# Opening transfers put in an order of their own, and the last norm of a diffusion trunk layer split over ScalarE and VectorE, on eight cores

## Time and profile before

| what | us |
|---|---|
| runs of the kernel before, median of 3 | 1055.67 (1051.9 to 1056.66) |
| the profiled execution | 1051.73 |
| its span on the slowest core (core 6) | 1049.8 |
| spans of the eight cores | 1039.6 to 1049.8 |
| PE matmul busy | 893.6 (85%) |
| DVE / POOL / ACT busy | 492.8 / 434.8 / 325.9 |

### The profile page before, as it was taken

The page is one execution under the profiler, slowest core; times in us unless marked ns, Lnnn a source line. Parts: engine busy times, 40 slices in busy tenths (PEclk is TensorE's granted clock), DMA queues, the critical chain, the costliest instruction groups (busy, mean ns, idle before and its releaser), DMA issues.

```text
span 1049.8 us, 15523 instructions; the slowest of 8 cores (1039.6 to 1049.8 us)
## 1 busy us (share of the span) xinstructions
PE 893.6 (85%) x5266; PEld 427.6 (41%) x5357; DVE 492.8 (47%) x979; ACT 325.9 (31%) x492; POOL 434.8 (41%) x411
## 2 busy tenths in 40 slices
PE   2136989877999998999989899979999999999970
PEld 1112544443444444444434444434444444444430
DVE  3134732776784227742477533322255433332380
ACT  1113745873782222762235421101112111111111
POOL 6033764312445235742576520033348633421055
PEclk9968999999999999999999999989999999999995
DMA  9995367452345668862768659986759875443027
GB/s 176 191 213 147 109 103 113 65 102 42 71 111 102 100 122 189 190 101 41 162 167 204 133 93 165 177 166 139 150 109 152 154 138 129 111 78 74 1 40 120
DMA packets 54636, 129.99 MB, mean 124 GB/s; under 512 B 5024, under 2 KB 6304, under 8 KB 54304
## 3 DMA queue, kind: packets, MB, share of 16 engines
q0 software_dynamic: 31584, 69.15, 41.7%
q1 hardware_dynamic: 22976, 59.86, 20.5%
HBM read 164.58 MB, written 16.78 MB: 173 GB/s over the span
## 4 chain that ended last, share of the span: by engine, by line
PE 58%; DMA 21%; issue 7%; DVE 6%; ACT 4%; POOL 2%; SPq 0%; DVEq 0%; POOLq 0%; ACTq 0%
PE psum L512 55%; DMA arena<-wff 6%; DMA arena<-wada 4%; DMA arena<-arena 4%; DMA arena<-xh 2%; DMA arena<-badabc 2%; DMA arena<-ctxb 2%; DMA out<-arena 1%; DVE arena L528 1%; DVE arena L524 1%; PE psum L710 1%; PE psum L676 1%; ACT arena L680 1%; ACT arena L777 1%; POOL arena L504 1%
## 5 line engine op out<-in xcount | busy, mean ns | idle before, releaser
L512 PE MATMUL psum<-arena 128*128 128x512 bf16 (+2 forms) x3704 | 806.5, 374 | 51.1 <-DVE arena L618 14.3
L512 PEld LDWEIGHTS psum<-arena 128*128 128x128 bf16 x3792 | 361.0, 99 | 472.6 <-issue 79.9
L806 POOL TENSOR_TENSOR arena<-arena 128x512 bf16<-128x512 f32 x88 | 113.6, 1302 | 187.6 <-DMA arena<-wff 149.5
L824 ACT ACTIVATE arena<-psum 128x512 f32<-128x512 f32 x88 | 52.4, 596 | 311.4 <-PE psum L512 311.4
L825 DVE TENSOR_TENSOR arena<-psum,arena 128x512 bf16<-128x512 f32 x88 | 60.8, 691 | 175.2 <-PE psum L512 166.4
L524 DVE BATCH_NORM_STATS2 arena<-arena 128x6 f32<-128x512 f32 x152 | 103.7, 689 | 73.2 <-DMA arena<-xh 31.5
L837 DVE TENSOR_TENSOR arena<-psum,arena 128x1024 f32<-128x1024 f32 x64 | 78.2, 1223 | 57.3 <-PE psum L512 57.2
L527 POOL TENSOR_TENSOR arena<-arena 128x1 f32<-128x1 f32 x84 | 51.3, 628 | 97.1 <-DVE arena L526 91.6
L749 DVE SCALAR_TENSOR_TENSOR arena<-arena,psum 128x512 f32<-128x512 f32 x64 | 43.7, 685 | 93.1 <-PE psum L512 89.4
L680 ACT ACTIVATE arena<-psum 128x1024 bf16<-128x1024 f32 x80 | 78.0, 1024 | 14.3 <-PE psum L676 12.8
L745 ACT ACTIVATE arena<-psum 128x512 f32<-128x512 f32 x64 | 38.1, 598 | 95.3 <-PE psum L512 95.2
(11 more groups left out here) (72 smaller groups left out, 566.0 us busy)
## 6 DMA issues: line engine op xcount, KB each, us to landing
arena<-wff SPq DMA_DIRECT2D x88, 256.0 KB, 4.9
arena<-wff POOLq DMA_DIRECT2D x22, 1024.0 KB, 10.8
arena<-xh SPq DMA_DIRECT2D x34, 512.0 KB, 7.0
arena<-wada POOLq DMA_DIRECT2D x24, 512.0 KB, 9.1
arena<-wc POOLq DMA_DIRECT2D x16, 768.0 KB, 8.3
arena<-arena POOLq DMA_DIRECT2D x16, 512.0 KB, 6.2
out<-ln2b SPq DMA_DIRECT2D x16, 512.0 KB, 35.6
out<-arena POOLq DMA_DIRECT2D x16, 512.0 KB, 7.0
```

Source lines behind the costliest of these rows:

```text
L512: r = e.matmul(out, lhsT=pairs[i][0], rhs=pairs[i][1], start=(i == 0), stop=(i == n - 1))
L806: G.op('pool', lambda e, fi=fi, hs=hs, stg=stg: e.tensor_tensor(out=w2[i % 5][:, fi, hs], in0=stg, in1=g2bc[:, hs], op=ALU.mult))
L824: G.op('act', lambda e: e.activation(out=sg, in_=ps[0], func=AF.Silu))
```

## The change

- The planner's prices (`cost`) and its hand-over times change for all engines, so that the order on each engine may change anywhere.
- Opening: wqk, perm and wu are issued right behind the w_ada blocks; x tiles 6 to 9 are read through the software queue; x tiles 4 and 5 no longer wait for the last w_ada block; wvb, wv, masks and wst follow. The second rope part waits for wu, the small loads and later x tiles and rope parts for wv or wst, the `wada1` blocks for wst. The context pair moves from group 0 to group 1.
- In late q and k units the permutation product goes to bank 5 (`bk_misc`) instead of banks 6 and 7.
- c2: ln1b is added by POOL instead of an accumulating DMA.
- Tail: the last accumulate is done in two half passes that also give row sums; ACT squares with the mean as bias and sums; two DVE passes apply mean, gain, scale and offset; SP stores the result. The 16 transfers that fill the output with ln2b go; ln2b is loaded once.

```diff
 def cost(self, eng, name, a, kw, out, ins):
-            return (1.0 if eng == 'pool' else 0.07)
+            return (0.8 if eng == 'pool' else 0.07)
...
-                    return 0.9
-                return 0.15 + n * 2.6 / 1200.0
-            return 0.15 + n * 1.05 / 1200.0
+                    return 0.56
+                return 0.18 + n / 472.0
+            return 0.34 + n / 1196.0
...
-                done = end + (0.2 if e == 'pe' else 0.1)
+                done = end + (0.25 if e == 'pe' else 0.15)
...
-    def qk_unit(m, hcol, n, dst, banks):
-        pq, ps = bk(banks())[:, 0:n], bk(banks())[:, 0:n]
+    def qk_unit(m, hcol, n, dst, banks, pbanks):
+        pq, ps = bk(banks())[:, 0:n], bk(pbanks())[:, 0:n]
...
-        G.op('pool', lambda e: e.dma_start(out=w, in_=ln1b, accum_op=ALU.add))
+        G.op('pool', lambda e: e.tensor_tensor(out=w, in0=w, in1=ln1b, op=ALU.add))
...
-    def tail(t):
+    def tail(t, b0):
+
         acc = xmid[t]
-        rstd, nmr = stats(acc, 1024)
-        y = y0[t % 3]
-        G.op('act', lambda e: e.activation(out=y, in_=acc, func=AF.Identity, scale=rstd, bias=nmr))
-        G.op('pool', lambda e: e.tensor_tensor(out=y, in0=y, in1=ln2g, op=ALU.mult))
-        G.finals.append(G.op('pool', lambda e: e.dma_start(out=out_d[t * 128:(t + 1) * 128, :], in_=y, accum_op=ALU.add)))
+        y = y0[t % 2]
+        s = st_i[0] % NST
+        st_i[0] += 1
+        st, mv = stt[:, s], mvr[:, s]
+        for h in range(2):
+            hs = slice(h * 512, (h + 1) * 512)
+            G.op('dve', lambda e, h=h, hs=hs: e.scalar_tensor_tensor(
+                out=acc[:, hs], in0=bk(b0 + h), scalar=1.0, in1=acc[:, hs], op0=ALU.mult, op1=ALU.add,
+                accum_out=st[:, h:h + 1]))
+        G.op('dve', lambda e: e.tensor_scalar(out=mv[:, 0:1], in0=st[:, 0:1], scalar1=st[:, 1:2], scalar2=-1.0 / D,
+                                              op0=ALU.add, op1=ALU.mult))
+        G.op('act', lambda e: e.activation(out=junk, in_=acc, func=AF.Square, bias=mv[:, 0:1], scale=1.0,
+                                           accum_out=st[:, 8:9]))
+        G.op('dve', lambda e: e.scalar_tensor_tensor(out=y, in0=acc, scalar=mv[:, 0:1], in1=ln2g, op0=ALU.add,
+                                                     op1=ALU.mult))
+        G.op('dve', lambda e: e.tensor_scalar(out=mv[:, 2:3], in0=st[:, 8:9], scalar1=1.0 / D, scalar2=EPS, op0=ALU.mult,
+                                              op1=ALU.add))
+        G.op('pool', lambda e: e.tensor_tensor(out=mv[:, 3:4], in0=mv[:, 2:3], in1=neghalf[:, 0:1], op=ALU.pow))
+        G.op('dve', lambda e: e.scalar_tensor_tensor(out=acc, in0=y, scalar=mv[:, 3:4], in1=ln2b, op0=ALU.mult,
+                                                     op1=ALU.add))
+        G.finals.append(load(out_d[t * 128:(t + 1) * 128, :], acc))
...
+    lq = cast_load(flat(wqk), wqk_d)
+    cast_load(perm, perm_d)
+    lu = cast_load(flat(wu), wu_d)
...
     a1_pair(0, 2, True)
     a1_pair(1, 4, True)
-    cast_load(flat(wqk), wqk_d)
-    cast_load(perm, perm_d)
-    cast_load(flat(wu), wu_d)
+    a1_pair(2, 6, True)
+    rope_load(0, 640, [wl])
+    for n in range(6, 10):
+        x_load(n)
+    rope_load(640, 1152, [lu])
     cast_load(flat(wvb), wvb_d)
...
-    a1_pair(2, 6, True, after=[wl])
...
+    lw = cast_load(flat(wst), wst_d)
+    load(esink, esink_d, after=[lv])
...
-        cast_load(flat(wada1[i % 2]), wada_d[ada[i]])
+        cast_load(flat(wada1[i % 2]), wada_d[ada[i]], after=[lw])
...
-            a1_pair(9, 6, False, after=[wl])
...
+            a1_pair(2 * g + 3, 6, False, after=[lv])
+            if g == 1:
+                a1_pair(9, 6, False, after=[lw])
...
-            o = G.ops[-1]
             load(ln2g, ln2g_d)
-            for t in range(NT):
-                G.op('sp', lambda e, t=t: e.dma_start(out=out_d[t * 128:(t + 1) * 128, :], in_=ln2b_d), after=[o])
+            load(ln2b, ln2b_d)
```

More of the change, by code:

```diff
@@ L33 @@
     __slots__ = ('id', 'eng', 'fn', 'deps', 'dur', 'lat', 'prio', 'dma', 'bytes', 'succ', 'npred', 'ready', 'pos',
[L34 removed]
+                 'need', 'vc', 'vdma', 'sem', 'semval', 'tick', 'est', 'last')
 class Rec:
@@ L97, in cost @@
         if name in ('dma_start',):
-            return (1.0 if eng == 'pool' else 0.07)
+            return (0.8 if eng == 'pool' else 0.07)
         n = self.free(out)
         ps_in = any(i.tensor.name == 'psum' for i in ins)
+        half_in = all(i.dtype == BF16 for i in ins if self.free(i) > 1)
         if eng == 'pe':
@@ L103, in cost @@
         if eng == 'act':
-            return (0.17 if ps_in else 0.21) + max(n, self.free(ins[0])) / 1200.0
+            if ps_in:
+                return 0.17 + n / 1200.0 + (n / 1350.0 if half_in else 0.0)
+            return 0.2 + max(n, self.free(ins[0])) / 985.0
         if eng == 'dve':
[L106 to L116, removed]
+            if name == 'bn_stats':
+                return 0.155 + self.free(ins[0]) / 960.0
+            fast = half_in and out.dtype == BF16 and name in ('tensor_tensor', 'tensor_copy')
+            fast |= name == 'tensor_scalar' and not ps_in
+            return (0.2 if name == 'scalar_tensor_tensor' else 0.155) + n / (1920.0 if fast else 960.0)
         if eng == 'pool':
@@ L342, in body @@
                     ins = o.fn(engine)
+                    o.last = ins.ins.name
                     if o.dma:
@@ L496, in build_nc @@
     actb = [at(x, BF16, FG, 1024) for x in (176, 150, 154, 50, 62, 66)]
-    y0 = [at(182 + 4 * i, F32, D) for i in range(3)]
+    y0 = [at(182 + 4 * i, F32, D) for i in range(2)]
+    junk = at(190, F32, D)
+    ln2b = at(166, F32, D)
     ln2g = at(194, F32, D)
@@ L575, in build_nc, with a1_pair @@
     tiles = [('x', i) for i in range(NTH)] + [('c', i) for i in range(2)]
-    def a1_pair(i, b0, split, after=()):
+    def a1_pair(i, b0, split, after=(), loads=True):
         which = 0 if tiles[2 * i][0] == 'x' else 1
@@ L582, in a1_pair @@
             src, dst = xr[n % NXR], xnb[n % 2]
-            load(src, (ctxb if which else xh)[ti * 128:(ti + 1) * 128, :], after=after)
+            if loads:
+                load(src, (ctxb if which else xh)[ti * 128:(ti + 1) * 128, :], after=after)
             rstd, nmr = stats(src, 1024)
@@ L620, in qk_unit, with k_unit, q_unit @@
         G.op('pool', lambda e: e.tensor_tensor(out=dst, in0=a, in1=b_, op=ALU.add))
-    def k_unit(g, banks):
+    def k_unit(g, banks, pbanks=None):
         n = 512 if g < 4 else 256
-        qk_unit(4, g * 512, n, kT[:, g * 512:g * 512 + n], banks)
-    def q_unit(m, g, banks):
-        qk_unit(m, 128 + g * 512, 512, qT[:, g, m, :], banks)
+        qk_unit(4, g * 512, n, kT[:, g * 512:g * 512 + n], banks, pbanks or banks)
+    def q_unit(m, g, banks, pbanks=None):
+        qk_unit(m, 128 + g * 512, 512, qT[:, g, m, :], banks, pbanks or banks)
     def v_unit(n, banks):
@@ L825, in gu, with dn @@
         G.op('dve', lambda e: e.tensor_tensor(out=ab(i)[:, fi, tok], in0=ps[1], in1=sg, op=ALU.mult))
-    def dn(rounds, t, b0):
+    def dn(rounds, t, b0, last):
         tk = slice((t % 8) * 128, (t % 8 + 1) * 128)
@@ L832, in dn @@
         acc = xmid[t]
-        if rounds[0] % NR == 0:
+        if last:
+            tail(t, b0)
+        elif rounds[0] % NR == 0:
             G.op('dve', lambda e: e.scalar_tensor_tensor(out=acc, in0=acc, scalar=ALPHA, in1=bk(b0, 2), op0=ALU.mult,
@@ L937, in build_nc @@
     B67 = Banks(6, 7)
-    k_unit(2, B67)
+    k_unit(2, B67, bk_misc)
     v_unit(8, B67)
@@ L945, in build_nc @@
         if g == 3:
-            k_unit(3, B67)
-            k_unit(4, B67)
+            k_unit(3, B67, bk_misc)
+            k_unit(4, B67, bk_misc)
         for m in range(4):
-            q_unit(m, g, B67)
+            q_unit(m, g, B67, bk_misc)
             v_unit(2 * g + 6 + m if g == 2 else 14 + m, B67)
@@ L1020, in build_nc @@
             t = 8 * half + q
-            dn(s, t, 2 if n < 2 or dn_i[0] % 2 == 0 else 4)
+            dn(s, t, 2 if n < 2 or dn_i[0] % 2 == 0 else 4, lastset)
             dn_i[0] += 1
-            if lastset:
-                tail(t)
             lo, hi = q * per, (q + 1) * per
```

30 lines of the change are left out of this document (14 added, 16 removed).

## The result

The kernel after takes 1021.81 us (median; 1020.17 to 1022.45) beside 1056.16 for the kernel before on the same chip: a ratio of 0.9685, 95% interval 0.9653 to 0.9718. The forecast was 1012, range 984 to 1040. The profiled execution has a span of 1019.6 on its slowest core (core 3), the eight cores 1013.9 to 1019.6.

What follows compares the result with a forecast made beforehand. PE was taken to bound the middle, something else both ends. Terms -15 - 2 - 4 - 8 + 1 - 14 = -42 from 1051.7 gave 1009.7; half of the median's 3.9 us excess was carried: 1012, range 984 to 1040.

Steps and rivals of the forecast that it cites:

- the port in c2: c2 passes: shared-port charge of +0.3 us on each of 32 scale steps, 10 us of DVE, 4 reaching PE.
- Opening, -15 forecast: Opening: reordered loads and the moved context pair save 15 us, bounds 0 and -27.
- the planner has no gap on POOL before them in which wvb could slip ahead: Opening: norm steps of tiles 0 to 3 fill POOL, so wvb cannot be issued before x6 and x7.
- the -6 for q_unit(0): Opening: q_unit(0) starts near 67 us against 73.38, a gain of 6.
- The gain behind the context pair: Opening: the 9.85 us hole behind pair 9 goes, since it moves to group 1: -10.
- the first rival: Opening stays as long, DVE's order again putting late tiles ahead of rope products: 1027, or 1038; chance 0.19.
- Attention, -2 forecast: Attention: only the order and a late unit's second PSUM bank change; -2 us, bounds -8 to +8.
- c2, -4 forecast: c2 passes: POOL additions replace accumulating DMAs; -8 by the row alone, -4 with the port, bounds -12 and +8.
- I take 8 of these 11.8 as gone: c2 passes: of PE's 8.7 us waiting for the second norm and 3.1 for an evacuation, 8 go.
- The slower rival: c2 passes: port makes nearly every L528 wait 2.37 us, +55 us of DVE, whole 1071; chance 0.04.
- FFN, -8 forecast, and middle tails, +1: FFN: without prefills the 6.40 us wff wait and 2 us of low clock go; half 0's tail costs +1.
- Last tail, -14 forecast: End: eight DVE blocks of 4.1 us and a 4.3 us store end at 1035.6 against 1049.8; bounds -15 and -3.

Runs made afterwards that it cites:

- e3: The kernel after with the planner's prices and hand-over times of the kernel before: 1032.39 us, ratio 0.9811.
- e1: The kernel after with wvb, wv, masks and wst held until tile 3's norm, so x6 and x7 are issued first: 1011.72 us, ratio 0.9623.
- e2: The kernel after with the permutation product of late q and k units back in banks 6 and 7: 1026.00 us, ratio 0.9747.
- e6: The kernel before with only the new tail, and ln2b loaded once instead of the 16 prefills: 1030.37 us, ratio 0.9801.
- e10: The kernel before with only ln1b's addition moved to GpSimd (POOL): 1058.76 us, ratio 1.0074.
- e4: The kernel after with ln1b added by an accumulating DMA again in c2: 1033.13 us, ratio 0.9832.
- e5: The kernel after with the 16 transfers that fill the output with ln2b put back: 1028.62 us, ratio 0.9772.
- e9: e1 with late q, k and v units spread behind attention blocks 0 to 7, permutation product in banks 6 and 7: 997.53 us, ratio 0.9499.
- e11: e9's spread units plus both opening edits (loads held; pair 3's statistics behind group 0's q units), on the kernel after: 996.29 us, ratio 0.9482.

## Why the prediction was right and wrong

**The whole.** The forecast sum was -42, the stages gave some -30. FFN and tails came out at the forecast, c2 2 us better, the opening 9 us worse and the attention 5 us worse. The time lies in the range, although the opening's mechanism failed and two of the terms that came out, the port in c2 and the last tail, did so partly by luck.

**Opening, -15 forecast, -3 to -6 measured: the step that failed is "the planner has no gap on POOL before them in which wvb could slip ahead".** wvb went out at 11.31 and wv at 23.66, ahead of x6 and x7, and the -6 for q_unit(0) became +4.3. The step holds under the old prices, as e3 shows, and failed because the new prices, which are themselves part of the change, gave another order; which of the prices does it was not tested. With their shapes, 2.10 and 0.52 MB of f32, the prediction's own arithmetic puts x6 at 2 + 20.4 / 0.309 = 68.0 and x7 at 71.4 us; DVE took them at 69.25 and 72.36. So the byte rate held to 1.3 us, and so did the order that the prediction gave DVE (late tiles ahead of the last modulation of pair 2 and of the rope products). e1 put the queue into the order that the prediction assumed, and gave 168.9 for the opening: 12 to 16 below the 181.3 to 184.9 of the old order. q_unit(0) then started at 69.4 (67 forecast), and the wait of wada1 for wst appeared at 76.58 (75.5 forecast). The gain behind the context pair came as forecast: from q_unit(0) to the attention the median core took 99.9 us, before 110.0. This is the first rival's mechanism, at a part of its price.

**Attention, -2 forecast, +1 to +3 measured.** Inside the bounds of 8. The mechanism that the text gave, bank 5, is worth some -3 by e2, so that part was right. What it put at nothing is the clock. PE's holes stayed (21.0 against 22.3), while its granted clock over the 138 us fell from 0.99 to 0.94, so the loss lies in PE's work at a lowered clock: over the whole stage its busy time is 182.1 to 183.5 us in the three kernels with the old order (before, e6, e10) and 183.8 to 184.5 in three with the new (after, e4, e5). e2 and e3 show that neither bank 5 nor the prices, each by itself, brought it: with either undone the attention was not shorter. e9 shows that the place of the late units is worth 12 us, most of it holes. They stand behind block 7 in the kernel before too (there seven of the nine permutation products between 186 and 280 us come after 246), so the room is likely there in both kernels, though the spread was not run on the kernel before. Which detail of the new order lowered the clock stays open.

**c2, -4 forecast, -6 measured: size nearly right, reason not.** The step "I take 8 of these 11.8 as gone" failed: the same two waits total 7.5 + 4.0 = 11.5 after. What went is smaller: holes of 13.1 instead of 16.0 us in the 212 us stretch, and PE's busy time in the stage, 196.0 instead of 199.0 us in the median core. And the edit was priced by itself, where e4 (-13) and e10 (+3) show that its worth changed sign with the order it was planned in. The charge for the port came out in size, by luck: the 32 steps grew by 30.96 - 20.75 = 10.2 us against 10, but the prediction laid this to the doubled POOL work, and e10 has that doubled work with a growth of 0.4. The rule named in the prediction, the Trainium skill's "SBUF — State Buffer", section "SBUF: two separate sides", gives the port to whichever operation starts first; the trace agrees for the other direction too: a 128x1 power on POOL that started 0.19 us into L861 took 1.51 us instead of its 0.55, to 0.4 us past that pass's end. The slower rival needed 1.35 us more for each step; 0.32 more was measured (0.97 against 0.65).

**FFN, -8 forecast, and middle tails, +1.** From the last c2 transpose to the last plain accumulate (996.25 before, 979.70 after) the profiled cores gave -8.05 for both together, and e5 gave 8.2 back with a wait of 6.00 for wff. The prefills were the cause, and the middle tails cost next to nothing.

**Last tail, -14 forecast, -13.7 measured** (profiled cores, from the start of the last plain accumulate, 996.25 before and 979.70 after, to the end of the span; the row of before stands below). Here two sizes were off and cancelled: a DVE block is 4.45 us (35.6 from 981.02 to 1016.62 for eight), not 4.1, through the accumulator reads (2 x 0.083) and wide passes of 1.28 instead of 1.22; the store lands in 2.7 us instead of 4.3.

```profile
996.25 1.22 DVE L837 TENSOR_TENSOR arena<-psum,arena 128x1024 f32<-128x1024 f32 x1 [0.50 <-PE psum L512]
```

**The prediction's own tests.** "No PE hole of 10 us" behind q_unit(0), no wff wait, L528 near 1 us (0.97) and half passes under 1 us held. q_unit(0) near 67 missed (77.71), and POOL's wait for wst until about 75 shows in e1 (76.58), not in the kernel after. One sign of being wrong came: "over 20 us of holes between 50 and 95" came true with 21.6, and it rightly marked the opening as the place of the error.

## What to carry to other kernels

When a planner fixes every queue's order, a load recorded behind another can still be issued ahead of it: before arguing with bytes, write down the issue order of each queue, since one 2 MB weight ahead of a tile moves everything behind it by its bytes over the rate. Price an edit together with the order that it will be planned in, for the same line was worth -13 or +3 us. And where an engine has holes in one stretch and a cluster of independent units further down, spread the units: here that was worth 12 us, some 8 of it holes, beside the 13.7 of the last tail.

## What the runs showed of the hardware

- A running sum on a DVE pass or an ACT pass is an instruction of its own: 0.083 us on DVE, 0.186 on ACT. The DVE pass itself is not slowed (0.687 with it, 0.685 without).
- A plain store of 512 KB landed in 2.7 us (median of 16). A load of the same size, ln2g, took 4.3, and no x tile of that size landed in under 3.4 in the kernel before or 3.6 after.
- A 128x1 operation on POOL was held by a wide DVE pass over two SBUF tensors (1.51 instead of 0.55 us, for two of 16), as one on DVE was by a wide POOL operation (2.30 against 0.15).
- The same planned order gave openings up to 3.6 us apart in the median core in different executions (before, e6, e10), while FFN and tails repeated to 0.1 us (after, e1, e4, e9, e11).
